# A two-block transformer layer in one kernel: inverse steps of the gated delta rule ahead of the next head's products, the residual's first two tiles loaded apart, and another order in the first stage and at the first heads of each attention

## The reference

```
# first block: attention of 12 query heads over 4 key/value heads (own tokens and context), plus a Fourier mix
h  = modulate(rmsnorm(x),   shift, scale)        # shift, scale = silu(c)    @ w_ada
hc = modulate(rmsnorm(ctx), shift_c, scale_c)    #                silu(c_ctx) @ w_ada
kc, vc = heads(hc @ w_kv);  p = h @ w_in
q = rope(rmsnorm(q)) * d**-0.5;  k = rope(rmsnorm(k))
attn = softmax(q @ [k, kc].T) @ [v, vc]
y  = sigmoid(g_a) * ((attn * silu(z_a)) @ w_pa) + sigmoid(g_b) * ((fourier(u_b) * silu(z_b)) @ w_pb)
x2 = rmsnorm(x + gate * (y @ w_out), final_g)
# second block: 16 heads of stick-breaking attention, 16 heads of the gated delta rule, then a gated MLP
u   = rms(x2) * (1 + scale1) + shift1;   proj = u @ w_in_2
o_a = stick_breaking(rms(q_a), rms(k_a), v_a)
q_b, k_b, v_b = silu(causal_conv(proj ...))      # q_b, k_b l2-normalised
m   = I + tril(beta * k_b k_b^T * decay, -1)     # chunks of 64 tokens
w_v, w_k = m^-1 (beta v_b), m^-1 (beta exp(g) k_b)
o_b = the rule's scan over chunks with w_v, w_k and the decays
x3  = x2 + gate1 * ((sigmoid(ga) * (o_a @ p_a) + sigmoid(gb) * (o_b @ p_b)) @ w_out_2)
u2  = rms(x3) * (1 + scale2) + shift2
out = x3 + gate2 * ((silu(u2 @ w_gate) * (u2 @ w_up)) @ w_down)
```

## Time and profile before

| | us |
|---|---|
| median of 3 runs | 2838.76 |
| lowest, highest | 2837.47, 2842.93 |
| the profiled execution: its own time | 2839.5 |
| the profiled execution: span from first to last instruction | 2837.7 |
| PE busy in the span | 2770.7 (98%) |
| DVE busy | 2048.5 (72%) |
| ACT busy | 1459.0 (51%) |
| POOL busy | 371.1 (13%) |
| mean granted clock of TensorE | 0.995 of full |

### The profile page before, as it was taken

One profiled execution on the slowest core, in us unless ns is written; L12 is line 12 of the kernel. 1 busy time (PEld: TensorE's weight loads), 2 busy tenths in 40 slices (PEclk: granted clock), 3 DMA queues, 4 the chain that ended last, 5 costly groups with the idle time before them and its releaser, 6 DMA issues.

```text
span 2837.7 us, 42907 instructions
## 1 busy us (share of the span) xinstructions
PE 2770.7 (98%) x16354; PEld 2389.4 (84%) x16354; DVE 2048.5 (72%) x3588; ACT 1459.0 (51%) x2415; POOL 371.1 (13%) x958
## 2 busy tenths in 40 slices
PE   7989999999999999999999999999999999999999
PEld 4678888888888888888888888888888888888888
DVE  3368877888887777778887887778877555555554
ACT  3365544444565666666666444545454444344443
POOL 0013310000001243433433230000000000000000
PEclk9999999999999999999999999999999999999999
DMA  8956668888865555555555678888856555555564
GB/s 324 329 176 212 221 212 285 296 295 292 293 177 182 164 173 176 180 169 175 171 173 182 204 233 266 282 304 283 277 176 228 190 181 193 192 185 187 191 196 141
DMA packets 183422, 621.84 MB, mean 219 GB/s; under 512 B 20256, under 2 KB 28720, under 8 KB 182448
## 3 DMA queue, kind: packets, MB, share of 16 engines
q1 hardware_dynamic: 173216, 605.62, 64.1%
q10 hardware_dynamic: 10000, 13.47, 1.5%
HBM read 612.70 MB, written 4.21 MB: 217 GB/s over the span
## 4 chain that ended last, share of the span: by engine, by line
PE 74%; DVE 10%; ACT 5%; DMA 4%; POOL 4%; issue 3%; SPq 0%; ACTq 0%; DVEq 0%
PE ps L96 74%; DVE wlo L111 3%; POOL small L111 2%; DMA raw<-in_w 2%; DVE acc L117 1%; POOL small L114 1%; ACT whi L102 1%; DVE c_y L117 1%; PE ps L99 1%; ACT sb_l L102 1%; ACT L105 1%; ACT act L102 1%; DMA xs<-in_xc 1%; DMA xc<-in_xc 0%; ACT sb_z L102 0%
## 5 line engine op out<-in xcount | busy, mean ns | idle before, releaser
L96 PE MATMUL ps<-act,whi 128*128 128x512 f32 (+1 forms) x6560 | 1662.1, 393 | 15.2 <-DVE p_x L111 7.6
L96 PEld LDWEIGHTS ps<-act,whi 128*128 128x128 f32 (+1 forms) x6560 | 1179.0, 189 | 234.3 <-ACT whi L102 16.1
L111 DVE TENSOR_TENSOR wlo<-raw,whi 128x1024 fp32r<-128x1024 f32 (+3 forms) x883 | 1038.2, 1185 | 16.5 <-ACT whi L102 12.1
L102 ACT ACTIVATE whi<-raw 128x1024 fp32r<-128x1024 f32 (+3 forms) x883 | 896.2, 1027 | 266.5 <-PE ps L96 105.9
L96 PE MATMUL ps<-act,wlo 128*128 128x256 f32 (+2 forms) x6416 | 976.2, 291 | 4.7 <-DVE wlo L111 4.7
L96 PEld LDWEIGHTS ps<-act,wlo 128*128 128x128 f32 (+1 forms) x6416 | 870.2, 190 | 63.7 <-DVE wlo L111 9.3
L117 DVE SCALAR_TENSOR_TENSOR acc<-raw,c_act,acc 128x1024 f32<-128x1024 f32 x210 | 268.1, 1277 | 0.0
L114 POOL TENSOR_SCALAR small<-small 128x2 f32<-128x2 f32 (+3 forms) x316 | 111.3, 352 | 979.9 <-DVE small L114 850.2
L111 POOL TENSOR_TENSOR small<-small 128x2 f32<-128x2 f32 (+1 forms) x460 | 182.0, 396 | 363.0 <-ACT u_u L102 328.7
L111 DVE TENSOR_TENSOR w_u<-w_u,ps 128x256 f32<-128x256 f32 x44 | 18.4, 420 | 99.4 <-ACT w_u L102 99.4
L111 DVE TENSOR_TENSOR w_g<-w_g,ps 128x256 f32<-128x256 f32 x44 | 18.3, 421 | 95.2 <-ACT w_g L102 95.2
(11 more groups left out here) (327 smaller groups left out, 2322.7 us busy)
## 6 DMA issues: line engine op xcount, KB each, us to landing
raw<-in_w SPq DMA_DIRECT2D x418, 512.0 KB, 4.7
raw<-in_w_mod SPq DMA_DIRECT2D x192, 512.0 KB, 5.4
raw<-in_w_gate SPq DMA_DIRECT2D x88, 512.0 KB, 4.2
raw<-in_w_up SPq DMA_DIRECT2D x88, 512.0 KB, 4.0
raw<-in_w_s SPq DMA_DIRECT2D x64, 512.0 KB, 6.3
raw<-in_w_out SPq DMA_DIRECT2D x64, 512.0 KB, 5.8
raw<-in_w_down SPq DMA_DIRECT2D x64, 448.0 KB, 4.5
raw<-in_w_ada SPq DMA_DIRECT2D x32, 512.0 KB, 4.9
```

What stands on the lines that cost most here:

```text
L96: return self.e.matmul(*args, **more)
L102: return self.e.activation(*args, **more)
L111: return self.e.tensor_tensor(*args)
```

## The change

It moves work and splits two transfers; it computes the same values by the same instructions but for one copy that goes from ACT to DVE.

- The input `xc` is loaded in pieces of 2, 4, 4, 4 and 2 tiles instead of four of 4.
- First stage: the activation table of logarithm and exponential is asked for before the wait on `norm_v`; the copy of the first modulation rows (`rows(0)`) goes from ACT to DVE; `columns(0)` stands before `normalise(0)`; in the loop `normalise(j)` stands after the first `lo_kv` of the previous group instead of before both; `pick(0)` stands before the rows of group 1, and every `pick(j)` from 2 on comes one `kv` unit earlier or two (j = 2).
- First attention: key head 3 is normalised and rotated in turn 9 instead of 8, and DVE does a turn's key work after its query work.
- Residual: `xs` is loaded as 2, 10 and 4 tiles; the first two epilogues of `out1` wait for the first.
- Stick-breaking heads 0 to 3: keys 2, 2, 1 and 2 turns later, scores 1, 1, 0 and 0 turns later, transposed values of heads 1 and 2 later by 1 and 4.
- Delta rule, on PE and DVE: the loop over the inverse's steps stands before the products and the transpose of the next head.
- MLP: the first two gates go from turn `E2 + 5` to `E2 + 10` and `E2 + 11`.

The diff, cut:

```
@@ Plan.build
-            self.base("stick", h, (e + 10, e + 19, e + 29, e + 38)[h] if h < 4 else self.end("sk", h) + 3)
-            self.base("turned", h, self.end("sv", h) + (2, 5, 3, 2)[min(h, 3)])
-            self.base("key", h, (e + 8, e + 18, e + 24, e + 34)[h] if h < 4 else self.end("sk", h) + 2)
+            self.base("stick", h, (e + 11, e + 20, e + 29, e + 38)[h] if h < 4 else self.end("sk", h) + 3)
+            self.base("turned", h, self.end("sv", h) + (2, 6, 7, 2)[min(h, 3)])
+            self.base("key", h, (e + 10, e + 20, e + 25, e + 36)[h] if h < 4 else self.end("sk", h) + 2)
@@ sp
-        for i in range(4):
-            e.dma_start(XC[:, 4 * i:4 * i + 4, :], src["xc"][:, 4 * i:4 * i + 4, :]).then_inc(*lands(f"xc_in{i}", "xc", i))
+        for i, kts in enumerate((slice(0, 2), slice(2, 6), slice(6, 10), slice(10, 14), slice(14, 16))):
+            e.dma_start(XC[:, kts, :], src["xc"][:, kts, :]).then_inc(*lands(f"xc_in{i}", "xc", i))
@@ pe
         e.wait_ge(*on("norm_v"))
+        pick(0)
         scale_rows(1, [0, 1])
-        pick(0)
         scale_rows(1, [2, 3])
...
-        kv(1, 0, 3, 4)
+        kv(1, 0, 1, 4)
         pick(2)
+        kv(1, 0, 2, 5)
...
-            kv(j - 1, 1, 2)
+            kv(j - 1, 1, 1)
             pick(j)
-            kv(j - 1, 1, 2, 2)
+            kv(j - 1, 1, 3, 1)
...
-            for h in due(t, "delta", 5):
...
-            for h in due(t, "delta", 7):
...
             for x in range(6):
                 for h in due(t, "delta", 11 + 2 * x):
...
+            for h in due(t, "delta", 5):
...
+            for h in due(t, "delta", 7):
@@ act
         copy(NROW[:, :], PS[5][:, :]).then_inc(*tell("act_start", "norm_rows"))
+        ln_table()
         e.wait_ge(*on("norm_v"))
...
-        rows(0)
...
-                if t == 2 * kvi + 2:
+                if t == 2 * kvi + 2 + 1 * (kvi == 3):
                     e.wait_ge(*on("kv_var", kvi))
                     rsqrt(KY[:, :], KSQ[kvi % 2][:, :], KW[:, :], "act_kv", ("kv", kvi))
...
-            for i, (last, kts) in enumerate((("pa", slice(0, 12)), ("pb", slice(12, 16)))):
+            for i, (last, kts) in enumerate((("pa", slice(0, 2)), ("pa", slice(2, 12)), ("pb", slice(12, 16)))):
...
-            if t == E2 + 5:
-                for k in range(2):
+            for k in range(2):
+                if t == E2 + 10 + k:
@@ dve
-        newton(NY[:, :], NV[:, :], NW[:, :], "dve_start", "n_in", ("norm",))
+        e.wait_ge(*on("s", 0, 3))
+        e.tensor_copy(ROWS[0][:, 0:256], PS[7][:, 0:256]).then_inc(*tell("dve_start", "rows", 0))
...
+        newton(NY[:, :], NV[:, :], NW[:, :], "dve_start", "n_in", ("norm",))
+        columns(0)
         normalise(0)
-        columns(0)
...
-        normalise(3)
         for j in range(3, 9):
             lo_kv(j - 1, 0)
+            normalise(j)
             lo_kv(j - 1, 1)
             columns(j)
             first_operands(j)
-            if j < 8:
-                normalise(j + 1)
...
-                        e.wait_ge(*on("xs", n // 12))
+                        e.wait_ge(*on("xs", 0 if n < 2 else 1 + n // 12))
```

More of the change, by code:

```diff
@@ L868, in pe @@
                     held[c + 1] = [("g_x", h, x + 1)]
+            for h in due(t, "delta", 5):
+                c = 2 * (h % 2)
+                claim(c)
+                claim(c + 1)
+                for label in (("g_kq", 0, h), ("g_kq", 1, h), ("g_sq", h)):
+                    e.wait_ge(*on(*label))
+                mm(PS[c][:, :], KQ[:, 0:128], KQ[:, :], True, True)
+                mm(both(PS[c + 1][:, 0:256]), KQ[:, 128:256], both(KQ[:, :])[:, :, 128:256], True, True)
+                mm(PS[c + 1][:, 256:257], GSQ[:, 0:128], one, True, True)
+                mm(PS[c + 1][:, 257:258], GSQ[:, 128:256], one, True, True).then_inc(*tell("pe_delta", "g_prod", h))
+                held[c] = held[c + 1] = [("g_sb", h)]
+            for h in due(t, "delta", 7):
+                c = 2 * (h % 2)
+                claim(c)
+                flip(PS[c][:, 0:128], SA[h % 2][:, 0:128]).then_inc(*tell("pe_delta", "g_flip", h))
+                held[c] = [("g_l0", h)]
             for h in due(t, "delta", 23):
@@ L1819, in dve @@
                 e.tensor_copy(PTB[h % 2][:, 2:4, :].rearrange("p a b -> p (a b)"), PS[3][:, :]).then_inc(*tell("dve_att", "q_pt", h, 1))
+            for kvi in range(4):
+                if t == 2 * kvi + 2 + 1 * (kvi == 3):
+                    kg, ks, y = KG[kvi % 2], KS[kvi % 2], KY
+                    e.wait_ge(*on("kv_swap", kvi))
+                    e.wait_ge(*on("k1_rest"))
+                    tt(kg[:, 0:256], kg[:, 0:256], K1[:, K_CT:K_CT + 256], ALU.mult).then_inc(*tell("dve_kv", "kv_cos", kvi))
+                    tt(ks[:, :], ks[:, :], K1[:, K_ST:K_ST + 256], ALU.mult).then_inc(*tell("dve_kv", "kv_sin", kvi))
+                    newton(y[:, :], KSQ[kvi % 2][:, :], KW[:, :], "dve_kv", ("kv", kvi), ("kv_root", kvi))
+                    tt(kg[:, 0:256], kg[:, 0:256], ks[:, :], ALU.add).then_inc(*tell("dve_kv", "kv_turn", kvi))
+                    e.wait_ge(*on("kv_turn", kvi))
+                    tt(KT[:, kvi, :], kg[:, :], y[:, :], ALU.mult).then_inc(*tell("dve_kv", "k_t", kvi))
             for n in due(t, "pa", 1):
@@ L1947, in dve @@
                 p.then_inc(*tell("dve_ba", "ba_g"))
-            for h in due(t, "delta", 5):
-                c, v = 2 * (h % 2), SM[4 + h % 2][:, 0:4]
-                ba, b2 = PS[c], PS[c + 1]
-                e.wait_ge(*on("g_prod", h))
-                if h > 1:
-                    e.wait_ge(*on("g_scaled", h - 2))
-                stt(GSQ[:, 0:128], ba[:, 0:128], 1.0, ident, ALU.mult, ALU.mult, accum_out=v[:, 0:1])
-                stt(GSQ[:, 128:256], b2[:, 0:128], 1.0, ident, ALU.mult, ALU.mult, accum_out=v[:, 1:2])
-                e.tensor_copy(v[:, 2:4], b2[:, 256:258]).then_inc(*tell("dve_delta", "g_diag", h))
-                e.wait_ge(*on("g_diag", h))
-                ts(v, v, 0.25, ALU.mult, EPS, ALU.add).then_inc(*tell("dve_delta", "g_var", h))
-                e.wait_ge(*on("g_decay", h))
-                if h > 1:
-                    e.wait_ge(*on("g_o", h - 2))
-                tt(both(SA[h % 2][:, :]), both(ba[:, :]), two(DT[:, 0:256]), ALU.mult)
-                tt(both(SB[h % 2][:, :]), both(b2[:, 0:256]), two(DT[:, 256:384]), ALU.mult).then_inc(*tell("dve_delta", "g_sb", h))
             for x in range(6):
@@ L1982, in dve @@
                         e.transpose(IT[h % 2][:, 0:128], picked(v, 2 * s, 1)).then_inc(*tell("dve_delta", "g_t", h, x + 1))
+            for h in due(t, "delta", 5):
+                c, v = 2 * (h % 2), SM[4 + h % 2][:, 0:4]
+                ba, b2 = PS[c], PS[c + 1]
+                e.wait_ge(*on("g_prod", h))
+                if h > 1:
+                    e.wait_ge(*on("g_scaled", h - 2))
+                stt(GSQ[:, 0:128], ba[:, 0:128], 1.0, ident, ALU.mult, ALU.mult, accum_out=v[:, 0:1])
+                stt(GSQ[:, 128:256], b2[:, 0:128], 1.0, ident, ALU.mult, ALU.mult, accum_out=v[:, 1:2])
+                e.tensor_copy(v[:, 2:4], b2[:, 256:258]).then_inc(*tell("dve_delta", "g_diag", h))
+                e.wait_ge(*on("g_diag", h))
+                ts(v, v, 0.25, ALU.mult, EPS, ALU.add).then_inc(*tell("dve_delta", "g_var", h))
+                e.wait_ge(*on("g_decay", h))
+                if h > 1:
+                    e.wait_ge(*on("g_o", h - 2))
+                tt(both(SA[h % 2][:, :]), both(ba[:, :]), two(DT[:, 0:256]), ALU.mult)
+                tt(both(SB[h % 2][:, :]), both(b2[:, 0:256]), two(DT[:, 256:384]), ALU.mult).then_inc(*tell("dve_delta", "g_sb", h))
             for h in due(t, "delta", 25):
@@ L2069, in dve @@
                         *tell("dve_ff", f"ff{half}", i))
-            if t == E2 + 5:
-                gate_silu(e, stt, 0)
-                gate_silu(e, stt, 1)
+            for k in range(2):
+                if t == E2 + 10 + k:
+                    gate_silu(e, stt, k)
     def gate_silu(e, stt, k):
```

31 lines of the change are left out of this document (3 added, 28 removed).

## The result

The changed kernel takes 2796.44 us (median of 4 runs, 2796.09 to 2797.95), against 2838.6 us before (2837.47 to 2842.93). The ratio is 0.985, 95% interval 0.9833 to 0.9867, so the change saves 42 us. The prediction said 2805, with a range from 2797 to 2819. The direction was right and the gain was there, but it was 42 us instead of 34, and the time lies 0.6 us under the range; of the four executions one, 2797.95, lies inside it.

What follows compares the result with a forecast made beforehand. PE was taken to bound the kernel, with only its 67 us of idle time to win at unchanged work. Six terms, 9.0 + 2.5 + 6.0 + 5.3 + 9.2 + 2.1 = 34.1 us off 2839.5, gave 2805 us, range 2797 to 2819.

Steps and rivals of the forecast that it cites:

- The clock: Half-clock stretches going with their stands: first stage 1.7 us, residual 2.2, stick-breaking heads 1.7; 5.6 us in all.
- What bounds the kernel: Whole kernel: PE busy 2770.7 of 2837.7 us, so 67 us idle to win; PE mostly waits for DVE, 72% busy.
- First stage: Start of kernel: stands for operands, picks and weight split go, with one half-clock stretch, 1.0 us given back; 9.0 us, 4 to 12.
- Key head 3: First attention heads: waits for `q_sq` and `prob` go, a new stand of some 2 us comes; 2.5 us, 1.2 to 5.
- Residual: Around 730 us: PE's 4.31 us stand and 2.2 us of half clock go; 6.0 us, 3.5 to 6.5.
- Rival 5: Residual: the split of `xs` does nothing for PE, the second piece lands late and stops DVE; 2811 us, chance 0.05.
- Stick-breaking heads: Heads 0 and 1: three stands and a half-clock stretch go, 0.5 us given back; 5.3 us, 2 to 9.
- rival 3: Second block and `prob_t`: more closes than aimed at, no new stand before `prob_t`; 8 us more, 2797 us, chance 0.10.
- Delta rule: 1000 to 1730 us: nine waits for `p_m`, 9.8 us, go but for 0.6 us; 9.2 us, 6 to 9.8.
- rival 4: Delta rule: slower, PE waits for a late `i_x`; above 2844.5 us needs 40 us in 15 meetings; chance 0.02.
- MLP: Before the MLP: PE's stand of 2.09 us for the operands goes; 2.1 us, 1 to 2.4.
- rival 2: Whole kernel: half-clock stretches stay or come at other places instead of going with their stands; 2811 us, chance 0.14.

Runs made afterwards that it cites:

- norm_only: Kernel before with only the first stage's norm multiplication moved behind the group's first weight split; 2833.99 us, ratio 0.9979.
- norm_pick: Kernel before with the norm behind the first weight split and column picks one unit of products earlier (two at group 2); 2829.27 us, ratio 0.9966.
- xs_again: Kernel before with only `xs` loaded as 2, 10 and 4 tiles, measured a second time; 2832.77 us, ratio 0.9978.
- stick_only: Kernel before with only keys, transposed values and scores of stick-breaking heads 0 to 3 at the later turns; 2832.2 us, ratio 0.9973.
- delta_only: Kernel before with only the inverse's steps ahead of the next head's products on PE and DVE; 2832.31 us, ratio 0.9974.
- rate_only: Changed kernel with later modulation weights loaded at 0.66 per turn in the projections and 0.5 in the merge stage, instead of 0.58; 2793.69 us, ratio 0.9843.
- xs_only: Kernel before with only `xs` loaded as 2, 10 and 4 tiles, first measurement, profiled execution disturbed; 2833.46 us, ratio 0.9982.
- start_only: Kernel before with all edits of the first stage and none of the others; 2827.43 us, ratio 0.9953.
- mlp_only: Kernel before with only the first two MLP gates moved to turns `E2 + 10` and `E2 + 11`; 2833.98 us, ratio 0.9985.
- key_only: Kernel before with only key head 3 one turn later, on DVE behind the query work; 2837.85 us, ratio 0.9997.
- prob_first: Changed kernel with ACT's copy `prob_t` ahead of the tanh; 2796.97 us, ratio to before 0.9857.
- more_moves: rate_only plus `prob_t` first on ACT and DVE, `v_tok` ahead of tanh and `whi` on ACT, stick-breaking softplus behind the inverse's step on DVE; 2786.72 us.

## Why the prediction was wrong by its range, and what in it was right

The mechanism came as described, except where `i_x` is late (below). The time is 8.6 us under the forecast because terms of the sum were mis-sized or left out. These steps failed; in the span they make 8.9 us:

- The clock (2.8 us): three stretches were counted as certain and all others as nothing. It gave 8.4 us instead of 5.6.
- Products behind a stand take longer (2.8 us): this term was put at nothing without a reason.
- Idle time (3.3 us): 31.8 instead of 28.5. The first stage gave 1.7 more, the stick-breaking heads 2.0 more and the merge stage, which no edit touches, 1.9; the delta rule gave 2.0 less and key head 3 1.2 less.

PE is idle for 35.3 us, inside the "about 35 to 40" that was named as a sign of being right. Four of the six terms ended above their own upper ends: 12.5 over 12, 6.6 over 6.5, 9.2 over 9, and 3.7 over 2.4.

**What bounds the kernel**: right. The gain is PE's idle time and what hangs on it, and DVE does the same work in a shorter time (73% busy instead of 72).

**First stage** (9.0 predicted, 12.5 measured). The six waits for `wlo`, the pick of group 2 and the last group's went as costed. Two steps failed for the idle time. The first is the 1.0 us that was given back to the memory: in the changed kernel only 0.6 us of waits for `w_s` are there, at 356 GB/s and 0.94, not far from the 361 worked out. norm_only shows that the danger was real (2.5 us), and norm_pick what lifts it: the picks. I had costed the picks by the products they pass and not by what DVE does with its head start. The second is that two short stands beside the aimed ones, of 0.32 us for `wlo` and 0.45 us for `mod` in the first groups, went as well and were left out of the sum. Of the clock 1.1 us more went, since the stretch at 27 us is 3.4 us long instead of 6.8. That is luck: the four other kernels with this first stage have 3.4 to 10.2 there.

**Key head 3** (2.5, 1.2): the mechanism was right, a new stand of 2.44 us where "some 2 us" was said. The size was the lower bound of its range, which was named for the case that came: a new half-clock stretch behind the new stand.

**Residual** (6.0, 6.6): right. The two tiles were there before DVE asked, no later piece stopped it, and the 6.5 us of the sum came without the deduction for shared transfers. Rival 5 is refuted by xs_again.

**Stick-breaking heads** (5.3, 9.2): the largest miss, and it lies just above "between 2 and 9". One term of the sum was too careful: of 2.8 us of stands I took 2.0, and all of it went. The 0.5 us given back came, as the wait of 0.6 us for `act`. The stands further on for `p_m` and `i_x`, which I had put only into the range and into rival 3, went from 3.2 to 1.9 us, and stick_only shows that these turns did it and not the delta rule's order. The last 1.7 us are the second half-clock stretch. In stick_only it is there, behind the same stand of 1.94 us, so its absence in the changed kernel is luck.

**Delta rule** (9.2, 7.9): for `p_m` "only what is longer than that stays" was right, 0.5 us where 0.6 was costed. The step that failed is that nothing else was set against the gain: three waits for `i_x` of 0.5 to 0.8 us came out, 2.0 us in all. They are in delta_only too. The edit's order is not to blame for more: rival 4 asked for 40 us.

**MLP** (2.1, 3.7): the stand went. I had left out the 0.34 us ahead of it, and the 1.3 us that the products behind both stands took longer.

**Not in the sum**: 1.9 us of the merge stage. It might as well have been a loss: the same stage has 0.6 us more idle time than before in norm_only and 1.2 in delta_only. What makes its stands is transfers, as far as rate_only and the rows beside it show; why it has fewer in the changed kernel isn't shown.

**The clock, rival 2**: the rival expected a loss, and the same chance worked the other way. I tied half clock to three stands, counted these three as certain and the others as nothing. In the trace of one execution a stand either has a stretch behind it or hasn't. Over the 13 traces of this case (that of xs_only is left out), behind the first 40 us:

| length of PE's stand, us | stands | with a half-clock stretch behind |
|---|---|---|
| 1.3 to 1.6 | 37 | 2 |
| 1.6 to 1.9 | 46 | 15 |
| 1.9 to 2.5 | 44 | 26 |
| 3.7 to 4.6 (the residual) | 8 | 8 |

At 1.7 us for a stretch, a stand of 1.9 to 2.5 us costs 1.0 us on average beside its length, and one of 1.6 to 1.9 us 0.6. The kernel before has five of the first sort and seven of the second, which makes some 9 us, and with the residual 11. Its trace has 11.6 in all, with the start. The changed kernel has two of the first sort behind 40 us, 2 us. This would have put the clock term at about 9 instead of 5.6, and the time at 2802. These shares come from the later traces. A view of one execution can't show it, but the places without a stretch in the earlier trace rows could have been read as chances and not as exceptions.

The single parts show the same from another side. Taking away one part's stands hardly lowers what half clock costs: it is 11.6 us in the kernel before, 8.8 in norm_only, and 11.7, 11.9, 12.3, 12.5, 12.8, 14.5 and 16.0 in stick_only, norm_pick, delta_only, start_only, mlp_only, xs_again and key_only. The stands left by each have stretches at other places in that execution. Only with nearly all gone does it fall, to 3.2, and to 1.7, 6.9 and 2.8 in prob_first, rate_only and more_moves. So the 8.4 us of the table are one draw as well. The six parts alone gain about 40 us by their ratios, each within some 3 us, so whether the whole is more than their sum can't be told from the times.

The stand before the MLP, 2.08 to 2.10 us long in all eight kernels that have it, has a stretch behind it in six. The Trainium skill (TensorE: Matmul & The Clock Gate, What's actually happening) says that the number of slow matmuls at a kernel's start differs between runs of one kernel. There is one trace of each kernel here, so no run repeats just that; the stretch at 27 us, 3.4 to 10.2 us long in five kernels with the same first stage, fits it.

**The range.** The lower end was put at the centre of rival 3 and not at its end. The upper bounds of the six terms add up to 44.7 us, which is 2795; terms that depend on the same thing (the clock, and how far DVE is in arrears) go wrong together, and four of the six did so upward. With the low end at 2795 the range would have held the time. Rival 3 named 2797 and "more closes than is aimed at" in the second block. That half came, 2.0 us of idle time at the stick-breaking heads. Its other half, no new stand before `prob_t`, didn't, and the clock and the slower products weren't in it; so its time was near the measured one partly by luck.

## What to carry to other kernels

Cost a stand of the bounding engine by more than its bracket: add the slower products behind it and a share of a half-clock stretch, by all stands of its length in the trace, not by whether this one has it. Where a wait names an engine, look at what that engine's queue, and the queue before that, were waiting for: the stands for `p_x` fell from 5.8 to 1.0 us when less was loaded beside them. When an order is turned so that one product of a chain comes earlier, ask which other member of the chain may now be the late one, and let the ends of a range reach to the case in which most terms err the same way.

## What the runs showed of the hardware

- Half clock (1.2 GHz) follows PE stands of 1.33 to 2.44 us in some executions and not in others, and it came with those of 3.7 to 4.6 us in all eight cases. Its stretches are 3.4 us long or a multiple (6.8, 10.2), but for those that the end of the kernel cuts off. Length isn't all: stands of 1.61 to 1.64 us before one product of the first delta-rule head had a stretch in 6 of 8 traces, those of 2.14 to 2.16 us at 1010 us in 1 of 8, and those of 1.68 us at 1110 us in none of 8. What else decides is open.
- Products right behind a stand at full clock take longer: 1.82 us for six instead of 1.56.
- Here is such a stretch in stick_only, behind the stand before the MLP, and then the kernel norm_only behind the same stand, where the clock stayed:

```profile
2109.20:2112.50 3.30, 3.30 (x11) 2.73 (x11) 3.12 (x7) 2.17 (x4) 0.00 (x0) 0.50 0.62 189
```

```profile
2108.00:2111.40 3.40, 3.40 (x21) 2.93 (x20) 3.22 (x7) 1.87 (x3) 0.00 (x0) 1.00 0.64 220
```

In the first PE finishes 11 products in the time in which it finishes 21 in the second, and both are "busy" throughout. The busy time doesn't tell them apart; the clock and the number of products do.
